# One token tile's gates added into a zeroed array by indirect DMAs, the gathered tile selected last, one-hot rows made in pieces inside the next selection

## The reference, cut to what matters

```
q = hf @ w_q                                   # 512 x (8 heads x 2 x 64)
scores = einsum(q, sub_keys)                   # per head 2 x 128 keys
sv, si = top_k(scores, 16); cand = sv0 + sv1   # 16 x 16 candidates
cv, ci = top_k(cand, 16); gates = softmax(cv)
e_idx = si0[ia] * 128 + si1[ib]
a = einsum(u_tab[e_idx], x)                    # first products
out = einsum(gelu(a) * gates, v_tab[e_idx])    # second products
```

## Time and profile before

| | us |
|---|---|
| median of 3 runs (lowest to highest) | 1857.47 (1855.21 to 1858.03) |
| the profiled execution | 1860.17 |
| its span | 1858.4 |
| PE busy in the span | 1683.6 (91%) |
| DVE busy | 1425.1 (77%) |
| ACT busy | 724.6 (39%) |
| POOL busy | 532.8 (29%) |

### The profile page before, as it was taken

The page is one execution under the profiler, slowest core; times in us unless marked ns, Lnnn a source line. Parts: engine busy times, 40 slices in busy tenths (PEclk is TensorE's granted clock), DMA queues, the critical chain, the costliest instruction groups (busy, mean ns, idle before and its releaser), DMA issues.

```text
span 1858.4 us, 23618 instructions
## 1 busy us (share of the span) xinstructions
PE 1683.6 (91%) x8496; PEld 1413.5 (76%) x8496; DVE 1425.1 (77%) x2754; ACT 724.6 (39%) x1068; POOL 532.8 (29%) x373
## 2 busy tenths in 40 slices
PE   3999779995998897997989999999989999998996
PEld 3886456774898897997989889989966667675765
DVE  7337999788289889989997789889874555545588
ACT  4433345433432324643665433433322333322332
POOL 2006970002032130050000357447434323231301
PEclk9999889997999998998999999999999999998998
DMA  7332223562243432664557899889889999998972
GB/s 279 130 103 91 91 91 114 181 209 97 81 159 125 167 134 74 250 234 163 198 203 256 294 373 351 312 324 382 281 287 331 359 331 340 343 369 281 349 253 97
DMA packets 172788, 422.24 MB, mean 227 GB/s; under 512 B 14976, under 2 KB 64256, under 8 KB 171136
## 3 DMA queue, kind: packets, MB, share of 16 engines
q1 hardware_dynamic: 132688, 256.08, 40.3%
q0 software_dynamic: 38256, 139.48, 20.1%
q10 hardware_dynamic: 1728, 25.17, 3.4%
HBM read 375.55 MB, written 45.09 MB: 226 GB/s over the span
## 4 chain that ended last, share of the span: by engine, by line
DVE 38%; PE 30%; DMA 14%; issue 6%; POOL 5%; ACT 4%; SPq 2%; DVEq 0%; ACTq 0%
PE bank L1585 9%; PE bank L1586 8%; PE bank L1587 8%; DMA gring<-gates_by_key 6%; POOL ring L583 5%; DVE conv L1061 4%; DMA vraw<-in_v_tab_dram 4%; DVE wlo L1228 3%; DVE one L1364 3%; DVE one L1362 3%; DVE one L1366 3%; DMA ring<-in_u_tab_dram,idxN 2%; PE bank L1872 2%; DVE wlo L927 2%; DVE ring L1233 2%
## 5 line engine op out<-in xcount | busy, mean ns | idle before, releaser
L1585 PE MATMUL bank<-act_hi,whi 128*128 128x384 f32 (+1 forms) x1352 | 486.8, 360 | 9.6 <-DVE act_lo L973 5.0
L1586 PE MATMUL bank<-act_lo,whi 128*128 128x384 f32 (+1 forms) x1352 | 474.5, 351 | 0.0
L1587 PE MATMUL bank<-act_hi,wlo 128*128 128x384 f32 (+1 forms) x1352 | 474.4, 351 | 0.0
L1585 PE MATMUL bank<-vhi,eh 128*128 128x512 f32 x768 | 309.1, 402 | 26.1 <-DVE vlo L1420 24.3
L1586 PE MATMUL bank<-vlo,eh 128*128 128x512 f32 x768 | 303.9, 396 | 0.0
L1587 PE MATMUL bank<-vhi,el 128*128 128x512 f32 x768 | 302.8, 394 | 0.0
L583 POOL DMA_INDIRECT ring<-in_u_tab_dram,idxN x128 | 196.1, 1532 | 332.3 <-DVE ring L1233 297.7
L1585 PEld LDWEIGHTS bank<-act_hi,whi 128*128 128x128 f32 x1352 | 257.9, 191 | 28.0 <-issue 11.2
L1420 DVE TENSOR_TENSOR vlo<-vraw,vhi 128x512 fp32r<-128x512 f32 x256 | 174.4, 691 | 127.1 <-ACT vhi L853 115.4
L1586 PEld LDWEIGHTS bank<-act_lo,whi 128*128 128x128 f32 x1352 | 257.4, 190 | 13.9
L1587 PEld LDWEIGHTS bank<-act_hi,wlo 128*128 128x128 f32 x1352 | 256.7, 190 | 13.3
(11 more groups left out here) (223 smaller groups left out, 2288.8 us busy)
## 6 DMA issues: line engine op xcount, KB each, us to landing
raw<-in_u_t_dram SPq DMA_DIRECT2D x128, 512.0 KB
vraw<-in_v_tab_dram SPq DMA_DIRECT2D x256, 256.0 KB
raw<-in_wblk_dram SPq DMA_DIRECT2D x61, 512.0 KB, 4.2
raw<-in_w_modt_dram SPq DMA_DIRECT2D x48, 512.0 KB, 3.4
gates_by_key<-stage ACTq DMA_DIRECT2D x12, 2048.0 KB, 7.5
gring<-gates_by_key SPq DMA_DIRECT2D x32, 768.0 KB
gelu_ahead<-gelz SPq DMA_DIRECT2D x20, 768.0 KB, 4.1
gback<-gelu_ahead SPq DMA_DIRECT2D x40, 384.0 KB
```

The costliest lines, as they stand in the source:

```text
L1585: mm(o, wh, mh, start=start, stop=False)
L1586: mm(o, wh, ml, start=False, stop=False)
L1587: return mm(o, wl, mh, start=False, stop=stop)
```

## The change

The stretch still has 80 chunks, now four steps of 16, 16, 24 and 24. The order of tiles is 1, 2, 3, 0.

- Tile 1, selected first, is no longer laid. Its indices are turned into flat cell numbers (two small DVE operations, with a token offset `tokF` made once), and its gates are put into the array by 128 indirect DMAs with an add (`scatter`), one for each of a token's 128 choices, 128 cells of 4 bytes each. They stand in POOL's queue: 19 beside the second selection, 48 beside the third, 4 and then 57 beside the fourth. Before each head's 16, all earlier ones must have landed. The cells are zeroed first: SP writes 8 DMAs of 1 MB from a zeroed tile, one after each of eight entries of the weight stream of sub-layer 1.
- Tiles 2 and 3 are laid within the selections of tile 3 and tile 0: their one-hot sets are made at points between the parts of the selection (`beside`), four buffers instead of two, and the token groups are spread over the step's PE units, from unit 32 of 192.
- The transposes of the selection stand 1.5 chunks into the next step (`SEL_UNIT`) instead of between two steps.
- POOL subtracts for 7, 7, 4 and 4 chunks instead of four times 7; DVE for the rest.
- Tile 0 is selected last, so its gathers are issued after it, after the last scatter and after the last token group (the ring lies where the one-hot buffers were). Its first dot is in the second chunk of the fill.
- SP and DVE wait for the landing of all 128 scatters before gates are read back.

```diff
-PRE_S, PRE_L, FILL = 14, 8, 8
-SPILL = TT * PRE_S + TD * PRE_L
+ORDER = (1, 2, 3, 0)
+STEPS = (16, 16, 24, 24)
+S_AT = (0, 16, 32, 56)
+FILL = 8
-DOT_F = (1, 1, 1, 1, 1, 1, 1, 1)
+DOT_F = (0, 1, 1, 1, 1, 1, 1, 2)
-SEARCHING = (0, 1, 2, 3, 4, 5, 7)
+SEARCHING = ((0, 1, 2, 3, 4, 5, 7), (0, 1, 2, 3, 4, 5, 7), (4, 5, 7, 8), (4, 5, 7, 8))
+LOWS = ((1,) * 16 + (0,), (1, 2, 1, 3, 1, 2, 1, 1, 1, 2, 1, 2, 1, 2, 1, 2, 0))
+ONES = (0, 2, 0, 2, 0, 2, 1, 1, 1, 1, 1, 1, 1, 1, 1, 1, 0)
+SEL_UNIT, GATE_LEAD = 12, 4
+SCATTERS = ((1,) * 6 + (13,), (1, 1, 1, 45), (1, 1, 1, 1))
+ZERO_AT = 2
...
@@ block.sync
+            first_zero = AT_STREAM[("w", O0 + ZERO_AT)]
             for s in range(s_f, len(STREAM)):
                 stream(s)
+                z = s - first_zero
+                if z == 0:
+                    sp.wait_ge(zero_r, 1)
+                if 0 <= z < 2 * (P // TB):
+                    part = gates_dram[z // 2, :, z % 2 * (NK // 2):(z % 2 + 1) * (NK // 2), :]
+                    sp.dma_start(part.rearrange("p (a i) t -> p a (i t)", a=4),
+                                 zeros[:].unsqueeze(1).broadcast_to([P, 4, HALF])).then_inc(zero_out, 16)
...
+            sp.wait_ge(gate_add, 16 * SLOTS)
@@ block.gpsimd
             def gather(j):
                 if j == 0:
-                    pool.wait_ge(sel_r, 1)
+                    pool.wait_ge(sel_r, TT)
+                    pool.wait_ge(gt_mm, NBT * LAID)
+            def scatter(n):
+                if n == 0:
+                    pool.wait_ge(sel_r, 1)
+                    pool.wait_ge(zero_out, 16 * 2 * (P // TB))
+                if n % TOPK == 0:
+                    need(pool, gate_add, 16 * n)
+                pool.indirect_dma_start(
+                    out=gates_flat, out_offset=bass.IndirectOffsetOnAxis(ap=selS[:, n:n + 1], axis=0),
+                    in_=selW[:, n:n + 1], in_offset=None, compute_op=ALU.add).then_inc(gate_add, 16)
@@ block.vector, in select(s)
+                def beside(point):
+                    if lays >= 0 and point == 1:
+                        transposed(s - 1)
+                    lows, ones = LOWS[lays >= 0][point], ONES[point] if lays >= 0 else 0
+                    for i in range(max(lows, ones)):
+                        if i < ones:
+                            one_hots(lays, made[1])
+                            made[1] += 1
+                        if i < lows:
+                            low_u(S_AT[s] + made[0] + 2)
+                            made[0] += 1
@@ block.tensor
+            def selecting(s):
+                lays = s - TT + LAID
+                for unit in range(STEPS[s] * KD):
+                    if lays >= 0:
+                        if unit == SEL_UNIT:
+                            sel_T(s - 1)
+                        for b in range(NBT):
+                            if GATE_UNIT[b] == unit:
+                                token_gates(lays, b)
+                    if s + 1 < TT and unit == STEPS[s] * KD // 2:
+                        retrieval_scores(s + 1)
+                    first_product(S_AT[s] + unit // KD, (unit % KD,))
```

More of the change, by code:

```diff
@@ L144, in build @@
         selT = sb("selT", [P, 3, P], F32, 199)
-        one = [sb(f"one{i}", [P, 2, WIDE, NK], F32, kb) for i, kb in enumerate((184, 112))]
+        one = [sb(f"one{i}", [P, 2, WIDE, NK], F32, 152 + 8 * i) for i in range(BUFS)]
+        selS = sb("selS", [P, SLOTS], I32, 190)
+        selW = sb("selW", [P, SLOTS], F32, 190.5)
+        zeros = sb("zeros", [P, HALF], F32, 132)
         ring = sb("ring", [P, RING, D], F32, 152)
@@ L590, in low_u @@
                                         ALU.subtract).then_inc(u_lo_pool, 1)
[L592 to L600, removed]
+            def scatter(n):
[7 more added lines that the diff above has]
+                    in_=selW[:, n:n + 1], in_offset=None, compute_op=ALU.add).then_inc(gate_add, 16)
+            for i in SEARCHING[0]:
+                low_u(S_AT[0] + i + 2)
+            scattered = 0
+            for s in range(1, TT):
+                for i, count in zip(SEARCHING[s], SCATTERS[s - 1]):
+                    low_u(S_AT[s] + i + 2)
+                    for n in range(scattered, scattered + count):
+                        scatter(n)
+                    scattered += count
+            for n in range(scattered, SLOTS):
+                scatter(n)
+            for j in range(SLOTS):
                 gather(j)
-            pool.wait_ge(selT_sb, 1)
+            pool.wait_ge(selT_sb, TT - 1)
             for n in range(P):
@@ L1291, in select @@
                 link(last)
-                while split[0] < 7:
-                    ahead()
+                beside(6)
                 best([cand[:, h, :] for h in heads], [cv[:, h, :] for h in heads],
-                     [pos[:, h, :] for h in heads], [cand2[:, h, :] for h in heads], lambda: None)
-                while split[0] < 8:
-                    ahead()
+                     [pos[:, h, :] for h in heads], [cand2[:, h, :] for h in heads], lambda point: None)
+                beside(7)
                 nc.vector.tensor_copy(posf[:], pos[:])
@@ L1367, in one_hots @@
                                         ALU.mult).then_inc(one_r, 1)
[L1369 to L1378, removed]
+            nc.vector.tensor_scalar(tokI[:, 1:2], tokI[:, 1:2], TB.bit_length() - 1, None, ALU.logical_shift_right)
+            link(nc.vector.tensor_scalar(tokI[:, 0:1], tokI[:, 0:1], TB - 1, None, ALU.bitwise_and))
+            link(nc.vector.tensor_copy(tokF[:, 0:2], tokI[:]))
+            link(nc.vector.tensor_scalar(tokF[:, 2:3], tokF[:, 1:2], float(P * NK * TB), tokF[:, 0:1],
+                                         ALU.mult, ALU.add))
             low_u(0)
             low_u(1)
[L1382 to L1393, removed]
+            for s in range(TT):
+                select(s)
             def weigh(g, k):
@@ L1794, in retrieval_scores, with sel_T, token_gates @@
                 last.then_inc(sc_mm, 1)
-            def sel_T(t):
-                pe.wait_ge(sel_r, t + 1)
+            def sel_T(s):
+                pe.wait_ge(sel_r, s + 1)
                 pe.wait_ge(xs_r, 2)
[L1799 to L1804, removed]
+                need(pe, selT_sb, s - 1)
+                need(pe, gt_sb, NBT * (s - TT + LAID))
+                for r in range(2 if ORDER[s] else 1):
+                    src = sel[:, r, :, :].rearrange("p h k -> p (h k)")
+                    last = nc.tensor.transpose(bank[2][:, r * P:(r + 1) * P], src, ident[:])
                 last.then_inc(selT_mm, 1)
-            def token_gates(t, b):
-                n = NBT * (t - 1) + b
+            def token_gates(l, b):
+                n = NBT * l + b
                 pe.wait_ge(one_r, n // 2 + 1)
@@ L1812, in token_gates @@
                 if b == 0:
-                    pe.wait_ge(selT_sb, t + 1)
-                row = one[n // 2 % 2]
+                    pe.wait_ge(selT_sb, l + 1)
+                row = one[n // 2 % BUFS]
                 for j in range(TOK):
```

180 lines of the change are left out of this document (92 added, 88 removed).

## The result

The changed kernel took 1844.97 us (median of 5 runs, 1842.73 to 1848.3) beside 1858.03 for the kernel before: a ratio of 0.9931, 95% interval 0.9916 to 0.9947. It is faster by 13 us; 36 were forecast. Its profiled execution took 1846.08 us, with a span of 1843.5.

What follows compares the result with a forecast made beforehand. DVE was taken to bound the stretch, with PE near; sub-layer 1's end and the fill were DMA chains. Terms -64 + 10 + 14 + 4 = -36 on 1860.2 gave 1824, median 1821 us, range 1795 to 1860.

Steps and rivals of the forecast that it cites:

- The stretch, -64: Selections and layings: one laying fewer, shorter waits and fewer POOL subtractions save 69 us, less 5 for interleaving; DVE's line 425.
- The 19.8 us: In the stretch: DVE's waits for ACT's rounding, which stands behind PE, 34.8 us less a first 15.0 before the stretch.
- the -8: In the stretch: saving taken from DVE's 19.8 us of waits for ACT, with ends of 0 and -19.8.
- the 71: In the stretch: two of the four steps take about 71 us each, the other two 140.
- The waits of 8.3 and 4.5 us: In the stretch: DVE waits 8.3 us for transposes (5.3 to be saved) and 4.5 for a free one-hot buffer (all saved).
- Rival 2: Stretch and fill: pieces interleave badly (+12 instead of 5), scatter tail 35 us instead of 19; -13, 1845 us; chance 0.14.
- The zero writes, +10: Sub-layer 1: 8.4 MB in SP's queue holds up the weights behind, delaying the first search 10 us; ends 0 and 22.
- The gathers' late start, +4: Fill: eight 512 KB gathers move into it, 11.9 us of transfers against 7.8 us of free DMA time; +4 (0 to 12).
- The scatters' tail, +14: Fill: scatters end 19 us after the last selection, delaying gathers, first dot and PE's subtractions; +14, ends 0 and +50.
- The 119 us: Beside the fourth selection: POOL's time for the last 57 scatters, against 100 us of room, so 19 us late.
- 57 x 2.3 + 26 = 157: Fourth selection: far bound for the last 57 scatters at 2.3 us each, 57 us late, +50.
- rival 3: Third step and fill: adding scatters take 3 us each and bound the kernel; +54, 1911 us; chance 0.12.

## Why the prediction was right or wrong

- **The stretch, -64: right in size** (-66.0), as were its steps, near 71 (593.11 to 665.10 us, the starts of two steps) and near 140. That the sum came out so well is in part luck, for its terms of waiting and of work missed in opposite directions. DVE's waits for ACT within the two stretches, before and after:

```profile
DVE wlo L1228 <- ACT whi L786: 13.4, 7, 4.1
DVE wlo L1271 <- ACT whi L836: 14.4, 8, 3.6
```

- The 19.8 us that the prediction took from the earlier trace rows reached beyond 998.93; in the stretch they were 13.4, and the -8 did not come. All of DVE's idle time fell by 8.3 us (33.0 to 24.7) and not by the 12.8 of its terms. Its work fell by 57.7 us (455.9 to 398.2), not by 51.2: the sets and the subtractions came as priced, but the products `eq` with `ecand` took 33.6 us instead of 37.7, and the conversions and sums of the indices (`sif`, `ecand`) 7.0 instead of 11.6. One such product of before took 3.08 us, and not the usual 1.05, beside a subtraction of POOL; the prediction had no term for this.
- The prediction also had DVE as the bound all along. PE bounds the first two steps: DVE's own sum for one, 57.4 + 9 x 1.14, gives 68, and the 71 stood in the prediction without a working. The waits of 8.3 and 4.5 us did go (1.3 is left, and none for a buffer), but the 4.5 through the pieces: four buffers gave nothing. Rival 2's other half, that the pieces interleave badly, did not come.
- **The zero writes, +10: 12.5**, by the mechanism named: SP's queue holds the last weights up and a chain runs from there. DVE's waits among them grew from 5.5 to 18.2 us, and the first search moved by all of it.
- **The gathers' late start, +4: at most 5.3**, by the run without the last 57 scatters.
- **The scatters' tail, +14: 33.3. This step failed**, and it is nearly the whole of the error (19.3 of 21.1 us in the span; the other three terms missed by 2.5, 1.3 and -2.0). The 119 us were 15 x 1.3 + 42 x 2.05 + 13. Measured: 41 scatters until the selection's end at 2.18 from start to start (89.5), 16 after it at 1.92 (30.7), 10.6 of waits for three landings beyond the usual gap of 0.30 (the 13 were enough), and 7.5 in two gaps that the profile calls "issue" and whose cause it doesn't show. That is 138.3. So the price of an issue failed, by 15 us, and the gaps added 7.5. The cheap ones I had priced by a gather's 0.94 and 1.03; with an add the least is 1.55. The room was smaller too: 94.4 us from the first of the 57 to the selection's end, not 100. So they were 43.9 us late instead of 19, and 10.6 of that was absorbed instead of 5.
- The mechanism was right: the queue order, the gather behind the last scatter, the dot in the fill's second chunk with the subtractions behind it. The prediction had named the bound for it, 57 x 2.3 + 26 = 157, and rival 2 at 2.3 us a scatter (35 us late) is close to what came, for the tail and not for the pieces; that its 1845 is the time measured is chance. Its fault was to take, for an operation that no row showed, the price of the nearest row in which only the direction of the transfer seemed to differ, where the add was new as well.
- Of rival 3 (3 us a scatter, a landing at a time) nothing came, but only just: the third step's 45 scatters took 115.0 us instead of 98, and POOL's next subtraction had 1.10 us of slack left (28.0 in the run with plain writes). Issue is the main price. A landing of 16 was waited for seven times, 29.8 us in all, 8.4 at most. The read-modify-write that the Trainium skill tells of ("DMA: Bandwidth & Descriptors", Specifications) may lie within those landings; no run here shows it apart. The 0.6 us of the add stand in POOL's issue, where that page's rule doesn't put them.
- The lock of the Trainium skill ("SBUF — State Buffer", SBUF: two separate sides) agrees in direction for scatters too: 1.55 us beside an idle DVE, up to 2.09 mostly beside its operations on two tiles. The section grants it to such an operation only against a GpSimd instruction that reads SBUF, and no run here shows that it is this lock that lengthens the issue. Without the longer issues the 41 would have cost 1.85 each, 14 us less in all; the forecast had that in. The add, 57 times 0.6, is 34 us, and the forecast had none of it.

## What to carry to other kernels

When a step goes into a queue, count from the queue's end: how much room it has until the next thing in it is wanted, and whether its own waits (here a landing after every 16) fall ahead of that. Work that fits by its sum can still stand in front of something: here the same 128 scatters cost 33 us or next to none by their place, and four of them moved too far cost 8 by the medians, 4 by the profiles. An operation with one more feature than the rows show, as an add, gets the far bound as its price, not the nearest row. A wait counts for a stretch only if it lies in it, and a sum that comes out right says little of its terms. And a bulk write belongs behind the last load of a chain, not among its loads.

## What the runs showed of the hardware

- An indirect DMA of 128 cells of 4 bytes costs POOL the same issue time as a gather of 128 rows of 4 KB: 0.95 us at least beside 0.94. With an add it is 1.55. Beside DVE operations that read two tiles both grow, a scatter with an add mostly by 0.5 (2.09), a gather by 0.8 to 1.0 (1.75 to 1.99).
- 8.4 MB written from a tile in one queue among 512 KB loads: the loads' time to landing is 6.2 and 9.5 us, beside 4.3 and 4.7 for the same two tensors in the kernel before, and the writes' is 11.2. Rows of DMA issues, 384 to 440 us, of the changed kernel (KB each, median us to landing):

```profile
gates_by_key<-zeros SPq DMA_DIRECT2D x8, 1024.0 KB, 11.2
raw<-in_wblk_dram SPq DMA_DIRECT2D x10, 512.0 KB, 6.2
raw<-in_w_modt_dram SPq DMA_DIRECT2D x6, 512.0 KB, 9.5
```

- PE's granted clock fell to 0.66 on average, partly its lower level (1.2 of 2.4 GHz), in the 50 us in which it mostly waited for the scatters' tail (window 950 to 1000), and was 0.89 from 1010 to 1056 us, where before it was 0.93.
